# Sample attention of a hybrid decoder step: products of four sequences issued in turn on four column groups, with eight slots for turned keys

## The reference, cut to what matters

```python
def fox_sample(q, k, v, lf, cache_k, cache_v, cache_lf, page_table):
    kp = cache_k[page_table].reshape(db, -1, H_F, DH_F)      # 8 sequences, 512 past rows, 8 heads of 64
    vp = cache_v[page_table].reshape(db, -1, H_F, DH_F)
    lfp = cache_lf[page_table].reshape(db, -1, H_F)
    past_cum = cumsum(lfp, axis=1);  f_past = past_cum - past_cum[:, -1:];  f_new = cumsum(lf, axis=1)
    lp = einsum('bthd,bshd->bhts', q, kp) * F_SCALE + f_new - f_past
    ln = einsum('bthd,bshd->bhts', q, k) * F_SCALE + f_new - f_new   # causal
    p = softmax(concatenate([lp, ln]))
    return einsum('bhts,bshd->bthd', p_past, vp) + einsum('bhts,bshd->bthd', p_new, v)
```

## Time and profile before

| what | value |
|---|---|
| median of three runs | 2408.08 us |
| span of the profiled execution (the page gives no time around it) | 2412.1 us |
| TensorE busy | 2153.4 us, 89% of the span |
| VectorE, ScalarE, GpSimd busy | 887.3, 534.4, 575.5 us |
| first group of the sample attention on TensorE | from 1048.38 us |
| second group | from 1117.14 us |
| first transfer of phase 5 | at 1184.91 us |

### The profile page before, as it was taken

The page is one execution under the profiler, slowest core; times in us unless marked ns, Lnnn a source line. Parts: engine busy times, 40 slices in busy tenths (PEclk is TensorE's granted clock), DMA queues, the critical chain, the costliest instruction groups (busy, mean ns, idle before and its releaser), DMA issues.

```text
span 2412.1 us, 32829 instructions
## 1 busy us (share of the span) xinstructions
PE 2153.4 (89%) x12219; PEld 1915.6 (79%) x12219; DVE 887.3 (37%) x1525; ACT 534.4 (22%) x845; POOL 575.5 (24%) x391
## 2 busy tenths in 40 slices
PE   2999997999789888678698999999999999999888
PEld 2877776999767777533287989999999999999688
DVE  3500001333256565511256324334344334343533
ACT  6222112222144444310153221100001100001311
POOL 1322102222021313110122233323232323230521
PEclk9999998988888999888899999999999999999899
DMA  3232215443222232362333112111111111110221
GB/s 116 70 107 84 81 42 170 135 134 99 77 62 61 70 74 70 99 206 72 117 135 107 35 44 62 46 41 45 42 45 42 52 35 52 35 35 7 66 68 36
DMA packets 203821, 179.36 MB, mean 74 GB/s; under 512 B 49114, under 2 KB 168126, under 8 KB 203746
## 3 DMA queue, kind: packets, MB, share of 16 engines
q1 hardware_dynamic: 154594, 151.28, 20.0%
q10 hardware_dynamic: 48160, 27.40, 4.0%
q0 software_dynamic: 1024, 0.13, 0.1%
HBM read 141.68 MB, written 39.26 MB: 75 GB/s over the span
## 4 chain that ended last, share of the span: by engine, by line
PE 77%; DVE 8%; issue 8%; ACT 2%; POOL 2%; DMA 1%; ACTq 1%; POOLq 1%; DVEq 0%; SPq 0%
PE pair L2078 22%; PE bank L2078 18%; PE bank L1807 8%; PE bank L1834 8%; PE pair L1807 4%; PE pair L1948 2%; PE pair L2028 1%; PE bank L2058 1%; PE pair L1922 1%; DVE dd L1451 1%; PE pair L1932 1%; PE pair L1921 1%; PE pair L2019 1%; DVE ptl L1498 1%; POOL tmp L935 1%
## 5 line engine op out<-in xcount | busy, mean ns | idle before, releaser
L2078 PE MATMUL bank<-acth,wha 128*128 128x352 f32 x640 | 213.1, 333 | 29.9 <-DVE actl L1630 17.2
L2078 PE MATMUL bank<-actl,wha 128*128 128x352 f32 x640 | 210.0, 328 | 0.0
L2078 PE MATMUL bank<-acth,wla 128*128 128x352 f32 x640 | 209.7, 328 | 0.0
L2078 PE MATMUL pair<-hh,whb 128*128 128x352 f32 x528 | 173.5, 329 | 24.2 <-DVE XR L1736 23.7
L901 POOL CAST wha<-raw 128x1024 fp32r<-128x1024 f32 x46 | 51.6, 1121 | 549.4 <-PE pair L2078 182.0
L1834 PE MATMUL bank<-acth,fwh 128*128 128x352 f32 x480 | 173.9, 362 | 3.7 <-POOL fwl L814 3.7
L2078 PE MATMUL pair<-hl,whb 128*128 128x352 f32 x528 | 169.2, 321 | 0.0
L2078 PE MATMUL pair<-hh,wlb 128*128 128x352 f32 x528 | 169.2, 321 | 0.0
L1834 PE MATMUL bank<-actl,fwh 128*128 128x352 f32 x480 | 166.7, 347 | 0.0
L1834 PE MATMUL bank<-acth,fwl 128*128 128x352 f32 x480 | 166.3, 346 | 0.0
L1736 DVE TENSOR_TENSOR XR<-XR,pair 128x352 f32<-128x352 f32 x264 | 134.2, 518 | 81.6 <-PE pair L2078 81.4
(11 more groups left out here) (420 smaller groups left out, 5156.8 us busy)
## 6 DMA issues: line engine op xcount, KB each, us to landing
raw<-in_w_gu SPq DMA_DIRECT2D x44, 512.0 KB, 3.8
wraw<-in_w_in SPq DMA_DIRECT2D x24, 512.0 KB, 4.7
scratch_zA<-stage SPq DMA_DIRECT2D x48, 256.0 KB, 2.0
raw<-in_w_down SPq DMA_DIRECT2D x22, 512.0 KB, 3.3
scratch_zT<-fout ACTq DMA_DIRECT2D x20, 528.0 KB, 2.7
fraw<-in_w_in SPq DMA_DIRECT2D x20, 512.0 KB, 3.9
gs<-scratch_zT SPq DMA_DIRECT2D x16, 528.0 KB, 3.6
kpg<-in_cache_k SPq DMA_DIRECT2D x32, 256.0 KB, 4.7
```

The lines of the kernel that those rows point to most:

```text
L2078: ins = nc.tensor.matmul(out, w[i](k), x[j](k), start=n == 0, stop=n == total - 1)
```

## The change

The edits are all in phase 4:

- the order of the 16 steps becomes s = 4c + b: first chunk 0 of all four sequences, then chunk 1, and so on;
- TensorE turns four steps, then issues the four products of the chunk before: T0..T3, T4..T7, L(0), T8..T11, L(1), T12..T15, L(2), L(3). The products of a chunk go to the four column groups in turn;
- the products with the forget values and the tail move out of the steps into `decays4`, behind L(3), and run over the four sequences in their inner loop; they signal a semaphore of their own (`ld4`), on which VectorE's maximum waits;
- `ktp` has eight slots in place of four and lies over `acth`, which is idle in this phase; the room it had stays reserved, so nothing else moves;
- the keys of sequence b in the next group are loaded after step 12 + b, its last one;
- the products with the values run page by page over the four sequences, then the four with the new values.

```diff
-        ktp = take("ktp", [P, 4, PAGES * PAGE])
+        ktp = at("ktp", attn_consts_end, [P, 2 * GB, PAGES * PAGE])
+        top[0] += GB * PAGES * PAGE * 4
...
-                    sp.wait_ge(kt_mm, g * 16 + 4 * b + 4)
+                    sp.wait_ge(kt_mm, g * 16 + 13 + b)
...
                 for s in range(0, 16, 2):
-                    act.wait_ge(l4_mm, 16 * g + s + 1)
+                    if s >= 8:
+                        act.wait_ge(l4_mm, 16 * g + s - 3)
+                    else:
+                        act.wait_ge(l4_mm, 16 * g + 4)
                     act.wait_ge(kt_mm, 16 * g + s + 1 + 16)
-                    nc.scalar.copy(ktp[:, s % 4, :], kt_bank(s)).then_inc(kt_a, 1)
+                    nc.scalar.copy(ktp[:, s % 8, :], kt_bank(s)).then_inc(kt_a, 1)
...
-                dve.wait_ge(l4_mm, 16 * g + 16 + 4)
+                dve.wait_ge(ld4, g + 1)
                 nc.vector.tensor_reduce(mx4[:, 0:1], pC[:, 0:PAGES * PAGE + NS], AX.X, ALU.max)
...
             def turn_keys(g, s):
-                b, c = s // 4, s % 4
+                c, b = s // GB, s % GB
...
+            def logits4(g, c):
+                n = PAGES * PAGE
+                for b in range(GB):
+                    s = c * GB + b
+                    pe.wait_ge(kt_d if s % 2 else kt_a, 8 * g + s // 2 + 3)
+                    nc.tensor.matmul(pC[rows4(b), 0:n], flat4(qz[:, c, b]), ktp[:, s % 8, :], start=c == 0, stop=False).then_inc(l4_mm, 1)
+
+            def decays4(g):
+                n = PAGES * PAGE
+                for i in range(PAGES):
+                    for b in range(GB):
+                        nc.tensor.matmul(pC[rows4(b), 0:(i + 1) * PAGE], flat4(lfr[:, b * PAGES + i]),
                                          sufm[:, (PAGES - 1 - i) * PAGE:], start=False, stop=i == PAGES - 1)
+                for k in range(4):
+                    for b in range(GB):
+                        nc.tensor.matmul(pC[rows4(b), n:n + NS], flat4(qz[:, k, b]), kT4[:, k, :], start=k == 0, stop=False)
...
             with pe.Fori(0, DB // GB) as g:
                 pe.wait_ge(grp_done, g + 2)
-                for s in range(16):
-                    turn_keys(g, s)
-                    if s >= 2:
-                        logits4(g, s - 2)
-                logits4(g, 14)
-                logits4(g, 15)
+                for c in range(4):
+                    for b in range(GB):
+                        turn_keys(g, c * GB + b)
+                    if c > 0:
+                        logits4(g, c - 1)
+                logits4(g, 3)
+                decays4(g)
...
+                for i in range(PAGES):
+                    for b in range(GB):
+                        nc.tensor.matmul(BANK[0][rows4(b), :], pT4[:, i, rows4(b)], vpg[:, b, i, :], start=i == 0, stop=False)
                 for b in range(GB):
-                    rows = slice(b * NS, (b + 1) * NS)
-                    for i in range(PAGES):
-                        nc.tensor.matmul(BANK[0][rows, :], pT4[:, i, rows], vpg[:, b, i, :], start=i == 0, stop=False)
-                    ins = nc.tensor.matmul(BANK[0][rows, :], pT4[0:NS, PAGES, rows], v4[:], start=False, stop=True)
+                    ins = nc.tensor.matmul(BANK[0][rows4(b), :], pT4[0:NS, PAGES, rows4(b)], v4[:], start=False, stop=True)
                 ins.then_inc(o4_mm, 1)
```

More of the change, by code:

```diff
@@ L432, in program @@
         l4_mm = sem("l4_mm")
+        ld4 = sem("ld4")
         nb4 = sem("nb4")
@@ L1597, in _ @@
                 for s in range(1, 16, 2):
-                    dve.wait_ge(l4_mm, 16 * g + s + 1)
+                    if s >= 8:
+                        dve.wait_ge(l4_mm, 16 * g + s - 3)
+                    else:
+                        dve.wait_ge(l4_mm, 16 * g + 4)
                     dve.wait_ge(kt_mm, 16 * g + s + 1 + 16)
-                    nc.vector.tensor_copy(ktp[:, s % 4, :], kt_bank(s)).then_inc(kt_d, 1)
-                dve.wait_ge(l4_mm, 16 * g + 16 + 4)
+                    nc.vector.tensor_copy(ktp[:, s % 8, :], kt_bank(s)).then_inc(kt_d, 1)
+                dve.wait_ge(ld4, g + 1)
                 nc.vector.tensor_reduce(mx4[:, 0:1], pC[:, 0:PAGES * PAGE + NS], AX.X, ALU.max)
@@ L2020, in turn_keys @@
                 ins.then_inc(kt_mm, 1)
[L2022 to L2029, removed]
-                    for i in range(PAGES):
-                        nc.tensor.matmul(pC[rows, 0:(i + 1) * PAGE], lfr[:, b * PAGES + i].rearrange("p h t -> p (h t)"),
-                                         sufm[:, (PAGES - 1 - i) * PAGE:], start=False, stop=i == PAGES - 1)
[L2033 to L2039, removed]
@@ new lines, in rows4, with flat4 @@
+            def rows4(b):
+                return slice(b * NS, (b + 1) * NS)
+            def flat4(x):
+                return x.rearrange("p h t -> p (h t)")
+            def logits4(g, c):
[4 more added lines that the diff above has]
+                    nc.tensor.matmul(pC[rows4(b), 0:n], flat4(qz[:, c, b]), ktp[:, s % 8, :], start=c == 0, stop=False).then_inc(l4_mm, 1)
@@ new lines, in decays4 @@
+            def decays4(g):
[3 more added lines that the diff above has]
+                        nc.tensor.matmul(pC[rows4(b), 0:(i + 1) * PAGE], flat4(lfr[:, b * PAGES + i]),
+                                         sufm[:, (PAGES - 1 - i) * PAGE:], start=False, stop=i == PAGES - 1)
+                for k in range(4):
+                    for b in range(GB):
+                        nc.tensor.matmul(pC[rows4(b), n:n + NS], flat4(qz[:, k, b]), kT4[:, k, :], start=k == 0, stop=False)
+                for b in range(GB):
+                    nc.tensor.matmul(pC[rows4(b), n:n + NS], flat4(lf4[:]), nmc[:], start=False, stop=False)
+                for b in range(GB):
+                    nc.tensor.matmul(pC[rows4(b), n:n + NS], flat4(sel[:, b]), maskq[:], start=False, stop=True)
+                for b in range(GB):
+                    ins = nc.tensor.matmul(pC[rows4(b), n + NS:n + NS + 1], flat4(lfq[:, b]), ones[0:NS, 0:1], start=True, stop=True)
+                ins.then_inc(ld4, 1)
```

## The result

The kernel after takes 2344.6 us (median of four runs, 2338.1 to 2350.3) against 2408.6 of the kernel before: a ratio of 0.972, 95% interval 0.969 to 0.975. The sign was right, the size was not: the time is near that of the rival "full overlap", 2345.5.

What follows compares the result with a forecast made beforehand. TensorE's own instructions were taken to bound both attention stretches. Savings of 3.8 + 16.2 = 20.0 us a group, 40 us for two, took the median from 2408.1 to 2368 us; range 2352 to 2403.

Steps and rivals of the forecast that it cites:

- full overlap: Rival, chance 0.08: second records hold nothing back, so products on four column groups run together; 31.3 us a group, 2345.5 us.
- What bounds the stage: In both sample attention stretches TensorE's own instructions set the time; a microsecond taken there comes off the kernel.
- Fewer changes of shape: Logits, values and tails on TensorE: fewer switches between 128- and 32-row shapes save 2.6, 0.7 and 0.5, 3.8 us a group.
- Products in turn: Logits, forget values and values over column groups: half overlap, chance 0.64, saves 5.2, 3.8 and 7.2, 16.2 us a group.
- No overlap: Rival, chance 0.16: streams of one shape go one by one whatever the columns; only 3.8 us a group, 2400.5 us.
- slower: Rival, chance 0.10: each change of column group empties the array, 0.115 us a product; 5.4 us lost a group, 2419 us.
- Waits and keys: Bank copies and the second group's later key loads cost nothing; five us of cover left at worst for the keys.

Runs made afterwards that it cites:

- lines apart: The kernel after with each sequence's product of the logits and of the values on its own source line, nothing else changed; 2344.9 us, ratio 0.973.
- new values last: The kernel before with its four new-value products moved behind all old-value products, each sequence on its own line; 2393.9 us, ratio 0.993.
- early preparation: The kernel after with VectorE's preparation of the second group moved ahead, to where TensorE works on the first group's values; 2339.2 us, ratio 0.971.

## Why the prediction was wrong, point by point

- *What bounds the stage*: right. TensorE's own instructions set it, and what they lost came off the kernel: 68.1 us from the first group's start to the second's last transposes in the two traces (132.2 to 64.1), 64 in the medians.
- *Fewer changes of shape, 3.8 us a group*: the direct price stands, 0.10 us where I had 0.115 (with lines apart the last values records start at 1068.88 and the new values at 1069.41, a record's 0.43 and 0.10 later). But the change to products over 32 rows costs more than its price. It is also the wall that keeps column groups from running side by side, and I priced it only as a delay. Moving four products out of the way gave 15 us where its price said 1.4.
- *Products in turn, 16.2 us a group*: this is the term that was mis-sized, and the step that failed is that a second record, waiting for its column group, holds back what is written behind it, since records "start in program order in every row". Second records do wait 0.43 us, but across column groups they hold nothing: a bunch of four spans 1.07 us where I said about 2.2. Logits, forget values and tail gave 21.0 us a group where I had 12.1, the values 13.4 where I had 7.9. The order that I saw in every row of before was that of one column group, or of products that a change of shape kept apart. It could not show the other.
- The Trainium skill, "TensorE: Matmul & The Clock Gate", "Part 3: Packing small matmuls": that products on other column tiles start beside each other agrees, 0.02 us for four. That they start strictly in program order does not hold here: 1048.18 behind 1047.75 with lines apart, and 1090.14 behind 1089.29 with the new values last. I had let the second sentence decide over the first.
- *Rivals*: full overlap, given 0.08, named the right mechanism. That it is right to 1 us in the median is partly luck: in the stretches it was low, 31.3 against 34.4 us a group. The tail overlaps too, 1.7 us a group where 0.5 was counted, and the other terms were each some 0.6 us low. *No overlap* and *slower* fell with the first bunch; changing column groups costs 0.007 us or so (1047.73 to 1047.75 for three changes), not 0.115.
- *Waits and keys*: cost nothing, as said; in early preparation the second group began 4 us earlier and the keys were there.
- *Range*: I let 0.64 rest on an order of starts that no row could test, and put the low end at 2352, above the 2345.5 of a rival that I had worked out myself.

## What to carry to other kernels

Float32 products of 32 output rows that write to different groups of 32 partitions ran side by side here, wherever no product of another shape stood between them: gather by shape first, then by turn. With products of two records each, two in a row to one group lost nothing, and four in a row did. And before a price is taken from rows, ask whether any row could have shown the opposite: where none could, that rival deserves an experiment or a larger chance.

## What the runs showed of the hardware that was not expected

- A float32 product is two records, and TensorE starts the halves of different column groups out of the written order (1047.73 to 1047.75 four firsts, 1048.18 to 1048.20 four seconds). It starts whole products out of it too (1089.29 ahead of 1090.14).
- In two runs, each column group held one running and three waiting records before what was written behind it was held up. Why three, whether it counts records or products, and whether other products count alike, stays open.
- A change between weights of 128 and of 32 rows is waited out by all column groups: sequences with such a product between them had no overlap, the same without it had (the stretch of the values fell from 20.3 to 12.0 us). For a change of columns alone, 128 against 32, no run shows this: a 128x128 transpose writes all 128 partitions, those of the four groups together, in any case.
